# 256 bytes instead of 128 between the weight slots and all other buffers

## The reference, cut to what matters

```python
z = h @ w_in                                  # attention, 2048 -> 4928
return (y * jax.nn.silu(gate)) @ w_out        # 2048 -> 2048
u, gate = jnp.split(h @ w_in, 2, axis=-1)     # Fourier, 2048 -> 8192
proj = jnp.einsum("bsd,dp->bsp", n, w_in)     # mixer, 2048 -> 13344
return jnp.einsum("bsm,md->bsd", mixed, w_out)
up = depthwise_conv_centered(jnp.einsum("bsd,df->bsf", n, w_ffn_in), conv_ffn_w)
return jnp.einsum("bsf,fd->bsd", jax.nn.silu(gate) * val, w_ffn_out)
```

## Time and profile before

| | us |
|---|---|
| median of 3 runs | 3235.32 |
| lowest and highest | 3231.34, 3259.40 |
| the profiled execution | 3227.28 |
| its span, first to last instruction | 3225.5 |
| mean granted TensorE clock in it | 0.969 |

### The profile page before, as it was taken

How to read it: one execution, slowest core, us unless ns; L and a number is a source line. 1 busy time by engine, 2 the same in 40 slices (tenths; PEclk the granted TensorE clock), 3 DMA queues, 4 the chain that set the end, 5 groups by cost and what they waited for, 6 DMA issues and landing times.

```text
span 3225.5 us, 52600 instructions
## 1 busy us (share of the span) xinstructions
PE 3071.2 (95%) x23262; PEld 2822.2 (87%) x23262; DVE 1855.3 (58%) x2132; ACT 1271.4 (39%) x1326; POOL 246.3 (8%) x244
## 2 busy tenths in 40 slices
PE   6999989988999999999999999998979999999998
PEld 3699775588988998989999989978879999999998
DVE  6746765466766434464544537755445667456653
ACT  7723331134433344343433425432233444344444
POOL 0001001000000000002112110032400000000000
PEclk8999999998999999989999989989989999999999
DMA  8746545354665553435444435500024555555553
GB/s 346 301 167 232 213 149 182 128 202 149 250 228 203 194 196 140 150 132 173 157 158 157 149 107 195 192 33 1 1 78 153 191 195 190 196 199 192 192 191 135
DMA packets 90850, 548.04 MB, mean 170 GB/s; under 512 B 10592, under 2 KB 10624, under 8 KB 45568
## 3 DMA queue, kind: packets, MB, share of 16 engines
q1 hardware_dynamic: 69408, 465.86, 40.4%
q0 software_dynamic: 18432, 67.12, 5.8%
q10 hardware_dynamic: 2784, 11.70, 0.9%
HBM read 542.54 MB, written 2.10 MB: 169 GB/s over the span
## 4 chain that ended last, share of the span: by engine, by line
PE 88%; DVE 5%; ACT 2%; issue 2%; DMA 1%; SPq 0%; DVEq 0%; ACTq 0%
PE bank L663 87%; DVE r L1812 2%; ACT r L1242 1%; DMA f<-in_units 1%; PE bank L725 1%; PE bank L994 0%; DVE f L1865 0%; DVE f L2351 0%; DVE f L2121 0%; ACT f L1359 0%; DVE f L1846 0%; DVE f L2240 0%; DMA f<-in_later 0%; DVE f L1988 0%; DVE f L2138 0%
## 5 line engine op out<-in xcount | busy, mean ns | idle before, releaser
L663 PE MATMUL bank<-r,r 128*128 128x256 f32 (+4 forms) x19360 | 2409.2, 287 | 62.3 <-DVE r L1812 31.3
L663 PEld LDWEIGHTS bank<-r,r 128*128 128x128 f32 (+3 forms) x19360 | 2297.4, 188 | 166.8 <-issue 76.3
L1812 DVE TENSOR_TENSOR r<-f,r 128x2048 fp32r<-128x2048 f32 (+2 forms) x466 | 1012.6, 2175 | 853.3 <-ACT r L1242 851.5
L1242 ACT CAST r<-f 128x2048 fp32r<-128x2048 f32 (+2 forms) x466 | 835.6, 1796 | 985.2 <-PE bank L663 803.3
L663 PE MATMUL bank<-f,f 128*128 128x128 f32 (+12 forms) x3390 | 639.4, 338 | 50.2 <-issue 7.3
L663 PEld LDWEIGHTS bank<-f,f 128*128 128x128 f32 (+6 forms) x3390 | 472.1, 196 | 161.5 <-issue 88.0
L1846 DVE SCALAR_TENSOR_TENSOR f<-f,f,f 128x512 f32<-128x512 f32 x240 | 180.0, 750 | 40.0 <-DMA f<-in_later 32.4
L2540 POOL DMA_DIRECT2D f<-in_later x128 | 67.8, 529 | 968.2 <-DVE f L1846 790.4
L1259 ACT COPY f<-bank 128x512 f32<-128x512 f32 (+2 forms) x141 | 80.2, 588 | 148.0 <-PE bank L663 142.5
L2289 DVE SCALAR_TENSOR_TENSOR f<-f,f,f 128x255 f32<-128x255 f32 (+1 forms) x272 | 131.7, 484 | 9.7
L2549 POOL TENSOR_TENSOR f<-f,f 32x512 f32<-32x512 f32 x24 | 30.9, 1289 | 735.5 <-PE bank L663 735.5
(11 more groups left out here) (205 smaller groups left out, 898.6 us busy)
## 6 DMA issues: line engine op xcount, KB each, us to landing
f<-in_units SPq DMA_DIRECT2D x346, 1024.0 KB, 4.8
f<-in_units SPq DMA_DIRECT2D x120, 768.0 KB, 4.3
f<-in_later POOLq DMA_DIRECT2D x128, 512.0 KB, 4.9
f<-in_units SPq DMA_DIRECT2D x8, 576.0 KB, 4.7
f<-in_x ACTq DMA_DIRECT2D x2, 1024.0 KB, 12.7
f<-in_ctx ACTq DMA_DIRECT2D x2, 1024.0 KB, 11.3
f<-in_x_turned ACTq DMA_DIRECT2D x1, 2048.0 KB, 11.1
f<-in_units SPq DMA_DIRECT2D x2, 800.0 KB, 4.4
```

The source lines that it names most:

```text
L663: return e.matmul(o, lhsT, rhs, start=start, stop=stop, skip_group_check=True)
L1242: e.copy(unit_view(high[HIGH_OF[u]][1], u), unit_view(raw[RAW_OF[u]][0], u)).then_inc(*up("w_hi", ("hi", u)))
L1812: e.tensor_tensor(unit_view(raw[RAW_OF[u]][1], u), unit_view(raw[RAW_OF[u]][0], u), unit_view(high[HIGH_OF[u]][1], u).bitcast(F32), ALU.su ...
```

## The change

The region `W` gets 64 floats beyond its slots instead of 32, and the slab becomes 32 floats longer, so that `R` keeps its size.

```diff
@@ -22,7 +22,7 @@
 HIGH = 3
 A_SCALE = (128 + 64) ** -0.5
 B_SCALE = 128 ** -0.5
-SLAB = 53132
+SLAB = 53164
 KEEP = 9360
@@ -485,7 +485,7 @@
-        W = Region(0, UNIT * (SLOTS + HIGH) + 32)
+        W = Region(0, UNIT * (SLOTS + HIGH) + 64)
         raw = [W.place(UNIT) for _ in range(SLOTS)]
         high = [W.place(UNIT) for _ in range(HIGH)]
         K = Region(W.size, KEEP)
```

## The result

The changed kernel takes 3284.21 us (median of 4 runs, 3278.09 to 3288.72), the kernel before, run beside it, 3244.49 us (median of 4, 3231.34 to 3259.40). The ratio is 1.0122, with a 95% interval of 1.0077 to 1.0168. That is slower by 1.2% (0.8% at least by the interval), and 3284 us lies above the stated range of 3215 to 3268 us. The medians differ by 40 us. The profiled execution took 3282.49 us, 55 us more than the profiled one of before (3227.28), which was quicker than all four of the runs beside it.

A forecast was written before the change was run, and what follows sets the result against it. TensorE was taken as the bound, through the interval between matmul starts. TensorE, VectorE with ScalarE, and transfers were each put at 0 us, so the sum of zero left the median at 3235 us, range 3215 to 3268.

The forecast's parts named there:

- What bounds the kernel: Whole kernel: TensorE, 88% of the chain; time is matmul count times the interval between starts, plus stalls.
- the three ways named: Whole kernel: the change can act only through matmul interval, duration of VectorE or ScalarE instructions TensorE awaits, or a transfer.
- The two intervals: Linear-layer matmuls: short, 113.3 ns between starts in the feed-forward stage; long, 117.8 ns in the output projection; 4.4 ns apart.
- 0 us for TensorE: Linear-layer matmuls: moving activations 128 bytes against the weight slots leaves their intervals unchanged, 0 us.
- which of them holds does not follow from the distance: Linear layers: short and long intervals both occur at either operand distance, as seen in `dv` and ordinary layers; 0 us.
- the distance in question: Ordinary linear layers after the change: 192 bytes modulo 256, counted from moving to stationary; `dv` had it before.
- With the same stalls it should come out the same: Linear-layer matmuls: a rhythm of weight loads and matmuls, set anew by stalls, should repeat unchanged; 0 us.
- The bounds: Linear-layer matmuls: all going long costs 80 us, the certainly short ones alone 38; all going short gains at most 42.
- the long interval takes over: Linear layers: stalls now end in the long interval, which holds for hundreds of matmuls; 62 us, 3297 us; chance 0.13.
- The head: Head units with a low weight half in the moved region, eight or nine: 117.7 against 113.3 ns; 2 us at most.
- VectorE, ScalarE and the transfers: Split units and transfers: other alignment costs nothing visible, 0 us; transfers mattering would be 1 or 2 us either way.
- the 3% fewer beats: Transfers of `later` pieces: by the descriptor rule, new alignment cuts 133 beats to 129, 3% less.

The follow-up runs named there:

- starts: Matmuls alone, reference not computed: 128 stretches of 96, eight start moments at each of four operand placements, then other trio orders; 113.3 ns or longer, no kernel time.
- sweep: Matmuls alone, reference not computed: 128 stretches of 96 over 32 activation distances, weights stationary or moving, with or without a wait; 113.3 to 120.0 ns with weights stationary.
- again: The kernel before, unchanged, run once more for a second trace: 3252.38 us.
- trio: Matmuls alone: high activations, low activations, low weights moved apart (tuples: their starts in bytes after the high weights); two of 64 combinations reached 113.3 ns.

## Why the prediction was wrong

**What bounds the kernel** was right: the chain's shares are the same within a point (VectorE 6% for 5), and the whole change went through the interval between matmuls, the first of the three ways named. **The two intervals** were read rightly, and 113.3 and 117.8 ns are the values of both kernels.

**The step that failed** is the one that took 0 us for TensorE, with the sentence "which of them holds does not follow from the distance". It rested on `dv`, which has the distance in question in the trace of before and runs at 113.3 ns in one place and 117.7 in another. From "both values occur at both distances" it went to "the distance doesn't matter", where it only shows that the distance alone doesn't decide. `starts` has exactly this: both values at both distances, in 6 and in 2 of 8 starts. A share would have said a little more than two stretches. In the trace of before, 831 of the 1,314 intervals of matmuls that move the weights were long (63%), and 3,225 of the 16,491 others (20%). Pricing those others at 63% gives some 7,200 more long ones, 32 us, 3267: the edge of the stated range, and right at the bound of 1%. But this sets layers of different stages side by side. Against its neighbours in the same stage `dv` was no worse: 0.62, with 0.63 in `dq` and `dk`. So the trace of before held no trial that could settle it; only a run with the distance changed could. It was a fair trial all the same, of the kind that `sweep` shows in its mirrored passes: with the distance of the changed kernel `dv` fell from 0.62 to 0.39, while `dq` and `dk` rose to 0.94 (the table above). (`oM` fell too, from 1.00 to 0.57 of its intervals, so the start had a hand in it there.)

**"With the same stalls it should come out the same"** failed as well, and for the unchanged kernel too: in `again` the feed-forward stage came out at 117.8 ns.

**The bounds** held: 38 to 80 us were the ends, and 53 us came between the two profiled executions, 40 us between the medians. **The rival that came true** is "the long interval takes over", in mechanism (a stage keeps for thousands of matmuls the rhythm in which it starts) and roughly in size (62 us and 3297 expected from 14,000 matmuls; 12,080 took part, and 3284 came). It was given 0.13, and its case against was again `dv`. Its condition, that the feed-forward stage tips, was right: that stage alone gave 24 us of the 55.

**The head** The earlier trace rows was the better witness, since there one operand of a trio stood elsewhere. Unit 40 has its low weights 192 bytes past its high ones, the point (192, 192, 192) of `trio`, which has 117.8 ns there too. I counted the head as 2 us because its units keep their distance, and didn't ask what it says of the other 18,000 matmuls.

**The Trainium skill** (SBUF — State Buffer, Who interferes with whom) has it that TensorE waits for no one. This speaks of other engines, and `sweep` doesn't contradict it, since there no other engine works. What it leaves out is TensorE with itself: the Trainium skill (TensorE: Matmul & The Clock Gate, Step-by-step: what each phase is for) says that its two read ports are independent and that loading the next weights takes no read bandwidth from the running matmul. If that were all that there is to it, all rows of `sweep` would have one length; they have 11.17 to 11.78 us. Whether it is bandwidth that is lost, no run shows.

**VectorE, ScalarE and the transfers** at 0 were right: 2.29 us and 4.8 and 4.9 us as before. The 4.9 us of `later` are now the same transfer at two alignments, and the 3% fewer beats worked out for it don't show. VectorE's wait for `in_later` went from 32.4 to 38.1 us, with no share in the result.

**What stays open.** That the two operands' starts act together is shown, and its period of 256 bytes, as is that the start of a stretch has a say. That they meet in the same part of the memory when a weight load and a matmul read at once would fit, but no run shows it. Nor is it known what in the moment of a start picks the interval; only that it does.

## What to carry to other kernels

A shift of a buffer that looks free was not free here, where TensorE is the bound: the distance between moving and stationary operand, modulo 256 bytes, is a parameter like any other, worth 3% here between the best and the worst. Look for more than one interval between equal matmuls at a full clock, and take out the stretches at the lower clock first. Don't conclude from single stretches or from a share across different stages that a distance doesn't matter; a run with one distance changed settles it. And when a kernel scatters by 1% from run to run, ask which of its stages changed rhythm before reading a difference of that size.

## What the runs showed of the hardware

- With `float32r` matmuls of 128 stationary and 256 moving columns back to back at a granted clock of 1.00, the interval is 113.3 ns at best. By the distance in steps of 32 bytes it is 120.0, 116.7, 117.8, 120.0, 118.7 to 120.0, 117.3 to 118.6, 113.3 (at 192) and 118.3 ns, with a period of 256 bytes (`sweep`, weights stationary). With the weights moving, the distances mirror: 64 has 113.3 ns there, or 117.8 by the start.
- Distances that aren't a multiple of 32 bytes are no better: in steps of 4 bytes between 144 and 236 they gave 116.0 to 121.6 ns (`trio`).
- Distances 192 and 64 have two steady intervals, 113.3 and 117.8 ns. Something in the start picks one, and it then holds for up to 5,776 matmuls (`again` against before). With weights stationary 192 was short in 6 of 8 starts, 64 in 2 of 8 (`starts`).
- Low weights 128 bytes off the high ones, at distance 192, came to 113.3 ns from all 8 starts, after seven to twelve long intervals (`starts`).
- By the Trainium skill (TensorE: Matmul & The Clock Gate, Wait — 56ns, not 53.3ns?) the interval is the columns at 2.4 GHz plus about 2.5 ns, an estimate of 109.2 ns for 256 columns. No stretch of these matmuls here comes under 113 ns on average.
